# An opening in pieces, block transposes through DRAM in both feed-forwards, and GpSimd as the issuer of their round trips

## The chip, the cores and the metric

The kernel runs on one core of a Trainium2 chip. The metric is the device time of one execution in microseconds (us). TensorE, VectorE, ScalarE, GpSimd and SyncE are the core's engines; each runs its own list of instructions in order and waits on semaphores.

## What is computed

Two transformer layers of batch 1, 256 tokens and width 2048, all in float32. The first: RMS norm, an attention of 16 heads with forget gates ("fox"), a residual, RMS norm, and a gated feed-forward with a causal convolution of width 3 over the tokens. The second: RMS norm, a mixer of two branches (a gated linear recurrence and a banded attention), a residual, RMS norm, a feed-forward with a squared ReLU, and a last norm. The parts that the change touches:

```python
def conv_ffn(h, w_up, conv_w, conv_b, w_down):     # D_FF = 5632
    up = h @ w_up                                   # 2048 x 11264
    padded = jnp.pad(up, ((0, 0), (2, 0), (0, 0)))
    y = conv_b + conv_w[0] * padded[:, 0:seq]
    for tap in range(1, 3):
        y = y + conv_w[tap] * padded[:, tap:tap + seq]
    gate, val = jnp.split(y, 2, axis=-1)
    return (jax.nn.silu(gate) * val) @ w_down

h = h + jnp.square(jax.nn.relu(u @ w_up[l])) @ w_down[l]   # second layer, D_FF_2 = 8192
```

## The kernel before, in words

All weights are streamed from HBM once, as 888 *slots*. A slot is 256 rows by 512 columns (a tile of 128 x 1024, 512 KB). SyncE loads it into one of four buffers `raw` (RING = 4); ScalarE rounds it to `w_hi` (`split`, line 827), VectorE makes the remainder `w_lo` (line 1221), and TensorE multiplies with both: per slot 2 token tiles x 2 row tiles x 3 products (hi x hi, lo x hi, hi x lo; lines 442 to 444) = 12 matmuls of 128 x 512. ScalarE and VectorE run AHEAD = 3 slots before TensorE: at program step p they split slot p + 3, ScalarE when TensorE has finished slot p - 1. SyncE issues a load when VectorE has split the slot four before. The order of everything else on an engine is written out by hand at steps p of each stage, so what stands behind a wait on ScalarE or VectorE are also the splits of later slots.

The activations must lie with the features on the partitions. TensorE turns them: `turn` (line 455) is a group of eight transposes of 128 x 128 into the PSUM banks 4 and 5 (`turn_ps`); `operand` rounds the result on ScalarE (859) and makes the remainder on VectorE (1231).

The *opening*: SyncE loads x in four chunks of 512 columns, each ahead of a slot. ScalarE issues the identity, a table with all gains and convolution taps (`tabs`), the fox gate weights (64-byte rows), a bias and the masks. TensorE turns the tables, then chunk 0 of x, waits for its operand, turns chunk 1, and starts the first slot. In the first fox pass ScalarE issues four DMAs that spread the gates over the partitions, one at each of steps 19 to 22.

*First feed-forward* (`ups1`, `downs`, `pass1`; 11 units of 512 hidden features). A pass of 24 slots is: 8 slots for the gate half of unit i into bank pair 0, 8 for the value half into pair 1, and 8 slots of the down projection of unit i - 1 (`downs`, four column chunks of two slots). Each half is evicted by ScalarE to `stage_q` and turned by TensorE, the gate at step 10 of its pass and the value at step 1 of the next. Then ScalarE computes one tap from PSUM (line 993), VectorE the other two (1395), ScalarE the sigmoid, VectorE the products (1414), and `gated` tells TensorE that the operand of the down projection is ready. In the last pass the value is turned at step 2 of the down slots, and eight more down slots follow for the last unit.

*Second feed-forward* (`ups2`, 16 units): a unit is 8 slots up and 8 slots of the down projection of the unit before. Here the turning is not TensorE's: ScalarE evicts with `by_block`, VectorE squares and transposes blocks of 32 x 32 (1604), one DMA writes 512 KB to DRAM (`turn_rows`) and four of 128 KB read it back with the blocks in place (`block_t`), and ScalarE (1165) and VectorE make the operand. SyncE issues these five DMAs between its weight loads (lines 392 and 401). The first unit uses bank pair 0, and TensorE waits for its eviction (`up2_out`) before the second unit.

GpSimd has little to do: the inverse roots of the norms, some fills, and three DMAs of 1024 KB.

Of the kernel before, what the change touches and what calls it, by code (L numbers as in the profile page):

```python
# [36 lines left out]
P = 128  # L37
# [76 lines left out]
def build_program(nc, a, out):  # L114
    with ExitStack() as ctx:
# [48 lines left out]
        D1_BANKS = [BK[0], BK[1], BK[0], BK[3]]  # L164
# [8 lines left out]
        ident_in, const_in, tab_in, f_kept = sem("ident_in"), sem("const_in"), sem("tab_in"), sem("f_kept")  # L173
        f_in, late_in, level_in, gain_in = sem("f_in"), sem("late_in"), sem("level_in"), sem("gain_in")
# [10 lines left out]
        z1_out, res1_out, up1_out, down1_out = sem("z1_out"), sem("res1_out"), sem("up1_out"), sem("down1_out")  # L185
        z2_out, merged_out, res2_out = sem("z2_out"), sem("merged_out"), sem("res2_out")
# [44 lines left out]
        TN_X, TN_RES1, TN_FFN1, TN_DOWN1 = 0, 4, 8, 8 + 2 * FFN1  # L231
# [67 lines left out]
        tabs = unit(8)[:, 0:5 * P].rearrange("p (k c) -> p k c", k=5)  # L299
        g_T, u_T, s_T = unit(1), unit(2), unit(3)  # L300
        v_pad = scratch[:, 2:4, :].rearrange("p t (h d) -> p t h d", d=P)
# [26 lines left out]
        def _(sp):  # L328
# [10 lines left out]
            def fox_body(R, g, first=False):  # L339
                for k in range(3):  # L340
                    for s in range(SPC):
                        p = k * SPC + s
                        if first and p < NCH:
                            c = slice(p * CW, (p + 1) * CW)
                            sp.dma_start(resid[:, :, c], x[:, :, c]).then_inc(x_in[p], 16)
                        load(R, p, a["w1"], s * SLOT_K * P, g * CW + k * D, wait=not (first and p < RING))
# [12 lines left out]
            def downs(R, p0, w, i, steps={}):  # L359
                for n in range(NCH):  # L360
                    for s in range(JT // SLOT_K):
                        if n * (JT // SLOT_K) + s in steps:
                            steps[n * (JT // SLOT_K) + s]()
# [23 lines left out]
            def turn2_out(i):  # L387

                sp.wait_ge(up2_block, i + 1)
                if i:  # L390
                    sp.wait_ge(up2_back, 64 * i)
                sp.dma_start(turn_rows, block_x).then_inc(up2_sent, 16)

            def turn2_back(i):

                sp.wait_ge(up2_sent, 16 * (i + 1))
                if i:
                    sp.wait_ge(up2_lo, i)
                rows = turn_rows.rearrange("(a p) (b e) -> b p a e", a=4, b=4)
                for b in range(4):  # L400
# [1333 lines left out]
```

## Time and profile before

| | us |
|---|---|
| median of three timed runs (2604.42 to 2606.49) | 2606.37 |
| the profiled execution | 2606.77 |
| its span, first to last instruction | 2604.8 |
| TensorE busy | 2573.1 (99%) |
| VectorE busy | 1596.4 (61%) |
| ScalarE busy | 1248.2 (48%) |
| GpSimd busy | 39.1 (2%) |
| moved by DMA | 495.41 MB, 190 GB/s |

Times in rows are us from the start of the span unless marked ns. PE is TensorE, DVE VectorE, ACT ScalarE, POOL GpSimd, SP SyncE; a q behind the name is the engine's sequencer, which issues DMAs. In a timeline a row is `start, duration, engine, line, operation, written<-read, count`, and in brackets the idle time of the engine before it and what ended it. Matmuls are pipelined: their shown durations overlap, so the distance of two starts tells more than a duration.

### The profile page before, as it was taken

How to read it: one execution, taken by the hardware profiler on the slowest of the kernel's cores; microseconds unless marked ns; L12 is line 12 of the kernel's file. 1: busy time of each engine (PE TensorE's matmuls, PEld its weight loads, DVE VectorE, ACT ScalarE, POOL GpSimd, SP SyncE). 2: the span in 40 equal slices, each digit the busy share in tenths (PEclk: the TensorE clock that was granted, in tenths of full speed). 3: DMA queues.
4: the chain of work that ended last, by engine and by line, in shares of the span. 5: the costliest groups of instructions: out<-in, count | busy, mean ns of one | idle time of the engine just before them, and what ended most of it. 6: DMA issues, size and time to landing. Idle time of an engine off the chain costs nothing.

```text
span 2604.8 us, 32206 instructions
## 1 busy us (share of the span) xinstructions
PE 2573.1 (99%) x11867; PEld 2141.5 (82%) x11867; DVE 1596.4 (61%) x1778; ACT 1248.2 (48%) x1586; POOL 39.1 (2%) x44
## 2 busy tenths in 40 slices
PE   7999999999999999999999999999999999999998
PEld 6888888888888888888888888888888888888886
DVE  4565555666666666675767555456556666666665
ACT  5555555545444444554343545444444444444444
POOL 0000000000000000000000000000000000000000
PEclk9999999999999999999999999999999999999999
DMA  6666555666656666656555655655577676767674
GB/s 199 219 181 174 169 164 176 198 188 187 186 185 191 185 181 186 187 182 186 160 155 164 192 171 163 181 190 186 186 224 220 211 224 213 221 210 224 208 225 157
DMA packets 259509, 495.41 MB, mean 190 GB/s; under 512 B 18060, under 2 KB 27108, under 8 KB 259300
## 3 DMA queue, kind: packets, MB, share of 16 engines
q1 hardware_dynamic: 254720, 486.60, 61.6%
q10 hardware_dynamic: 4019, 4.58, 0.5%
q0 software_dynamic: 688, 3.15, 0.4%
q8 instruction: 51, 0.84, 0.1%
q14 instruction: 31, 0.25, 0.0%
HBM read 483.76 MB, written 10.51 MB: 190 GB/s over the span
## 4 chain that ended last, share of the span: by engine, by line
PE 98%; ACT 0%; DVE 0%; ACTq 0%; DMA 0%; issue 0%; POOL 0%; POOLq 0%; SPq 0%
PE acc L442 31%; PE acc L444 31%; PE acc L443 31%; PE acc L455 2%; PE acc L672 1%; PE acc L515 1%; PE acc L522 0%; DMA raw<-in_w 0%; ACTq L885 0%; PE acc L532 0%; PE acc L544 0%; DVE w_lo L1221 0%; ACT w_hi L827 0%; PE acc L545 0%; PE acc L699 0%
## 5 line engine op out<-in xcount | busy, mean ns | idle before, releaser
L1221 DVE TENSOR_TENSOR w_lo<-raw,w_hi 128x1024 fp32r<-128x1024 f32 x888 | 1080.6, 1223 | 835.8 <-ACT w_hi L827 834.1
L827 ACT ACTIVATE w_hi<-raw 128x1024 fp32r<-128x1024 f32 x888 | 935.8, 1059 | 1060.1 <-PE acc L444 1038.4
L442 PE MATMUL acc<-w_hi,A_hi 128*128 128x512 f32 x1952 | 772.3, 396 | 2.2 <-ACT scratch L837 1.1
L444 PE MATMUL acc<-w_hi,A_lo 128*128 128x512 f32 x1952 | 761.2, 390 | 0.0
L443 PE MATMUL acc<-w_lo,A_hi 128*128 128x512 f32 x1952 | 761.0, 390 | 0.0
L444 PEld LDWEIGHTS acc<-w_hi,A_lo 128*128 128x128 f32 x1952 | 366.9, 188 | 77.2
L442 PEld LDWEIGHTS acc<-w_hi,A_hi 128*128 128x128 f32 x1952 | 367.2, 188 | 76.5 <-issue 1.7
L443 PEld LDWEIGHTS acc<-w_lo,A_hi 128*128 128x128 f32 x1952 | 367.3, 188 | 73.1
L442 PE MATMUL acc<-w_hi,B_hi 128*128 128x512 f32 x800 | 313.6, 392 | 1.5 <-ACT scratch L1181 1.5
L444 PE MATMUL acc<-w_hi,B_lo 128*128 128x512 f32 x800 | 311.5, 389 | 0.0
L443 PE MATMUL acc<-w_lo,B_hi 128*128 128x512 f32 x800 | 311.3, 389 | 0.0
L442 PE MATMUL acc<-w_hi,C_hi 128*128 128x512 f32 x800 | 311.3, 389 | 0.0
L444 PE MATMUL acc<-w_hi,C_lo 128*128 128x512 f32 x800 | 311.2, 389 | 0.0
L443 PE MATMUL acc<-w_lo,C_hi 128*128 128x512 f32 x800 | 311.2, 389 | 0.0
L442 PEld LDWEIGHTS acc<-w_hi,B_hi 128*128 128x128 f32 x800 | 150.2, 188 | 32.5 <-issue 1.9
L444 PEld LDWEIGHTS acc<-w_hi,B_lo 128*128 128x128 f32 x800 | 150.2, 188 | 31.3
L444 PEld LDWEIGHTS acc<-w_hi,C_lo 128*128 128x128 f32 x800 | 150.2, 188 | 31.1
L442 PEld LDWEIGHTS acc<-w_hi,C_hi 128*128 128x128 f32 x800 | 150.2, 188 | 31.1
L443 PEld LDWEIGHTS acc<-w_lo,C_hi 128*128 128x128 f32 x800 | 150.2, 188 | 31.1
L443 PEld LDWEIGHTS acc<-w_lo,B_hi 128*128 128x128 f32 x800 | 150.3, 188 | 30.7
L1249 DVE TENSOR_TENSOR resid<-resid,acc 128x1024 f32<-128x1024 f32 x116 | 141.5, 1220 | 37.9 <-PE acc L444 37.9
L837 ACT ACTIVATE scratch<-acc,small 128x512 f32<-128x512 f32 x108 | 69.3, 686 | 73.8 <-PE acc L444 73.7
(160 smaller groups left out, 1095.3 us busy)
## 6 DMA issues: line engine op xcount, KB each, us to landing
raw<-in_up SPq DMA_DIRECT2D x304, 512.0 KB, 4.5
raw<-in_w SPq DMA_DIRECT2D x272, 512.0 KB, 4.0
raw<-in_down SPq DMA_DIRECT2D x216, 512.0 KB, 4.1
raw<-in_wo SPq DMA_DIRECT2D x64, 512.0 KB, 4.1
raw<-in_wa SPq DMA_DIRECT2D x16, 512.0 KB, 4.9
raw<-in_wb SPq DMA_DIRECT2D x16, 512.0 KB, 4.6
turn_rows<-scratch SPq DMA_DIRECT2D x16, 512.0 KB, 6.5
scratch<-turn_rows SPq DMA_DIRECT2D x64, 128.0 KB, 3.7
```

Source lines behind the costliest of these rows:

```text
L442: pe.matmul(o, hi[:, kt, ts], wh, start=first and kk == 0, stop=False)
L443: pe.matmul(o, hi[:, kt, ts], wl, start=False, stop=False)
L444: m = pe.matmul(o, lo[:, kt, ts], wh, start=False, stop=last and kk == SLOT_K - 1)
L455: m = pe.transpose(turn_ps[:, j * T + t * P:j * T + (t + 1) * P], src(t, j), ident)
L515: m = pe.matmul(o, q[:, t * P:(t + 1) * P], k[:, 0:(t + 1) * P], start=True, stop=True)
L672: m = pe.matmul(o[:, c], s[:, c], t[:, c], start=True, stop=True)
L827: act.activation(w_hi[:, q % RING, :], raw[:, q % RING, :], ACT.Copy).then_inc(w_hi_ready, 1)
L837: m = act.activation(dst[:, t * CW:(t + 1) * CW], acc[:, banks[t], :], func, scale=scale[:, t:t + 1])
L1221: dve.tensor_tensor(w_lo[:, q % RING, :], raw[:, q % RING, :], f32(w_hi[:, q % RING, :]), ALU.subtract).then_inc(w_lo_ready, 1)
L1249: dve.tensor_tensor(v, v, acc[:, banks[0]:banks[1] + 1, :], ALU.add).then_inc(done, 1)
```

## The change

1. *Opening.* Only the 16 rows of the first gain are loaded and turned first; x chunk 0 and slot 0 come in two halves each and ahead of all else; ScalarE and VectorE work on them tile by tile (`early_split`, `early_operand`), and the first slot (`gemm_first`) runs in two halves with two transposes' worth of chunk 0 between them. Chunks 1 to 3 are turned at steps 1 to 3 (before: ahead of the first slot, and at steps 0, 2, 4), the tables at step 4. The fox gate weights, bias and constants are loaded later. The gates are spread by one DMA at step 19 and three at steps 0, 2, 4 of the next pass.
2. *First feed-forward.* The 22 groups of transposes on TensorE go. ScalarE evicts with `by_block`; VectorE transposes 32 x 32 blocks (`turn_blocks`), at step 8 for the gate and behind the split of step 16 for the value; GpSimd issues one DMA out and four back; ScalarE copies the result into place (`up_f`) and the taps are computed from there. The gate's taps move from step 10 to 14. The value's stay at step 1 of the next pass, but at step 5 in the second pass, and in the last pass they move from step 2 to 5 of the down slots. The down projection uses the bank pairs 2 and 3 alone.
3. *Second feed-forward.* GpSimd issues the round trips in place of SyncE. The first unit uses bank pair 3, so TensorE no longer waits for its eviction.

The diff, cut:

```diff
-        D1_BANKS = [BK[0], BK[1], BK[0], BK[3]]
+        D1_BANKS, D1_LAST = [BK[2], BK[3], BK[2], BK[3]], [BK[0], BK[1], BK[0], BK[3]]
...
+            def first_loads():
+                h = CW // 2
+                sp.dma_start(resid[:, :, 0:h], x[:, :, 0:h]).then_inc(x_early, 16)
+                sp.dma_start(raw[:, 0, 0:CW], a["w1"][0:P, 0:CW]).then_inc(w_early, 16)
+                sp.dma_start(raw[:, 0, CW:2 * CW], a["w1"][P:2 * P, 0:CW]).then_inc(landed[0], 16)
+                sp.dma_start(resid[:, :, h:CW], x[:, :, h:CW]).then_inc(x_in[0], 16)
...
+            def gemm_first():
+                for kk in range(SLOT_K):
+                    pe.wait_ge(early_hi, kk + 1)
+                    pe.wait_ge((w0_hi, w_hi_ready)[kk], 1)
...
+                    if kk == 0:
+                        pe.wait_ge(x_in[0], 16)
+                        turn_pair(2, turned)
+                m.then_inc(slot_done, 1)
...
+                if p in (1, 2, 3):
+                    pe.wait_ge(x_in[p], 16)
+                    turn(chunk_of_resid(p), TN_X + p)
+                if p in (2, 4):
+                    pe.wait_ge(turn_dve, TN_X + 1 + p // 2)
+                if p == 4:
+                    turn_tabs()
...
-                    elif p == 1:
-                        pe.wait_ge(up1_out, 2 * i)
-                        turn(halves(stage_q), TN_FFN1 + 2 * i - 1)
-                    if p == 10:
-                        pe.wait_ge(up1_out, 2 * i + 1)
-                        turn(halves(stage_q), TN_FFN1 + 2 * i)
+                    elif p % SPC == 0:
+                        pe.wait_ge(up1_out, 2 * i - 1 + p // SPC)
...
+                        if isinstance(g, int) and p in (0, 2, 4):
+                            spread_gates(1 + p // 2)
...
+            def conv_tap(i, half, dst):
+                n = 2 * i + half
+                act.wait_ge(up1_back, 64 * (n + 1))
...
+                act.activation(up_f.rearrange("p (m a q) -> p m a q", m=JT * TT, a=4), from_quads(up_t),
+                               ACT.Copy).then_inc(up1_flat, 1)
...
-                    if p == 10:
+                    if p == 14:
...
-                if q == 2:
+                if q == 5:
                     act.wait_ge(gated, FFN1 - 1)
                     conv_value(FFN1 - 1)
...
+            def turn_blocks(n, first=False):
+                dve.wait_ge(up1_out, n + 1)
+                if not first:
+                    dve.wait_ge(up1_sent, 16 * n)
+                dve.transpose(up_x, up_q).then_inc(up1_block, 1)
...
+                    if p == SPC:
+                        turn_blocks(2 * i, first)
...
-            downs(R4 - 4, 0, D1_BANKS, down1_out, steps=lambda q: value_steps(q - 2, FFN1 - 1, B_hi, B_lo))
+            downs(R4 - 4, 0, D1_BANKS, down1_out, steps=lambda q: value_steps(q - 5, FFN1 - 1, B_hi, B_lo),
+                  turn=2 * FFN1 - 1)
...
+            for n in range(2 * FFN1):
+                pool.wait_ge(up1_block, n + 1)
+                if n:
+                    pool.wait_ge(up1_back, 64 * n)
+                pool.dma_start(up_rows, up_x).then_inc(up1_sent, 16)
+                pool.wait_ge(up1_sent, 16 * (n + 1))
+                if n:
+                    pool.wait_ge(up1_flat, n)
+                for b in range(4):
+                    pool.dma_start(up_t[32 * b:32 * (b + 1), :].rearrange("p (a e) -> p a e", a=4),
+                                   up_by_quad[b]).then_inc(up1_back, 16)
...
+            for i in range(FFN2):
+                pool.wait_ge(up2_block, i + 1)
...
+                pool.dma_start(turn_rows, block_x).then_inc(up2_sent, 16)
```

## Rows read from the trace of the kernel before

**Rows 1.** The page: busy time of TensorE, and the last chain by engine.
```profile
PE 2573.1 (99%) x11867; PEld 2141.5 (82%) x11867; DVE 1596.4 (61%) x1778; ACT 1248.2 (48%) x1586; POOL 39.1 (2%) x44
...
PE 98%; ACT 0%; DVE 0%; ACTq 0%; DMA 0%; issue 0%; POOL 0%; POOLq 0%; SPq 0%
```

**Rows 2.** Stretches: busy time per engine, clock, DMA share, GB/s.
```profile
81.80:94.80 13.00, 13.00 (x59) 10.78 (x58) 6.34 (x5) 4.28 (x5) 0.44 (x1) 1.00 0.99 363
529.50:596.60 67.10, 67.10 (x306) 55.73 (x305) 43.59 (x47) 33.12 (x38) 0.00 (x0) 1.00 0.61 187
2047.90:2091.40 43.50, 43.50 (x193) 36.05 (x192) 27.45 (x23) 19.10 (x19) 0.00 (x0) 1.00 0.71 206
```

**Rows 3.** Waits of TensorE, whole run: total us, times, longest.
```profile
PE acc L468 <- DMA scratch<-in_rows: 8.6, 1, 8.6
PE acc L455 <- DVE A_lo L1231: 6.3, 1, 6.3
PE acc L442 <- ACT scratch L1181: 1.5, 1, 1.5
```

**Rows 4.** Timelines of the opening: ScalarE, VectorE, TensorE.
```profile
11.08 1.28 ACT L888 ACT_TABLE_LOAD   x1 [11.08 <-issue]
...
14.12 1.55 ACT L859 ACTIVATE A_hi<-acc,gain 128x256 fp32r<-128x256 f32 x4
...
15.70 1.66 DVE L1231 SCALAR_TENSOR_TENSOR A_lo<-acc,gain,A_hi 128x256 fp32r<-128x256 f32 x4 [0.23 <-ACT A_hi L859]
...
19.10 0.78 PE L442 MATMUL acc<-w_hi,A_hi 128*128 128x512 f32 x1
...
22.66 0.41 PE L444 MATMUL acc<-w_hi,A_lo 128*128 128x512 f32 x1
...
39.05 0.39 PE L442 MATMUL acc<-w_hi,A_hi 128*128 128x512 f32 x1
```

**Rows 5.** DMA issues: count, KB each, median us to landing.
```profile
const<-in_const ACTq DMA_DIRECT2D x1, 64.0 KB, 4.7
...
turn_rows<-scratch SPq DMA_DIRECT2D x16, 512.0 KB, 6.5
scratch<-turn_rows SPq DMA_DIRECT2D x64, 128.0 KB, 3.7
...
scratch<-in_rel POOLq DMA_DIRECT2D x2, 1024.0 KB, 7.8
...
scratch<-in_gain_out POOLq DMA_DIRECT2D x1, 1024.0 KB, 4.8
```

**Rows 6.** Timeline of TensorE at the two late starts.
```profile
96.40 0.50 PE L442 MATMUL acc<-w_hi,A_hi 128*128 128x512 f32 x1 [1.15 <-ACT scratch L837]
...
1917.19 0.49 PE L442 MATMUL acc<-w_hi,B_hi 128*128 128x512 f32 x1 [1.48 <-ACT scratch L1181]
```

**Rows 7.** Timelines of VectorE and SyncE, one trip of the second feed-forward.
```profile
2116.03 1.25 DVE L1604 STREAM_TRANSPOSE scratch<-scratch 128x1024 f32<-128x1024 f32 x1
...
2126.57 1.75 SPq L401 DMA_DIRECT2D scratch<-turn_rows  x4
```

**Rows 8.** Groups by line, ScalarE and VectorE: count, busy us, mean ns.
```profile
L1165 ACT ACTIVATE C_hi<-scratch 128x1024 fp32r<-128x1024 f32 x12 | 12.5, 1042 | 0.0
...
L1395 DVE SCALAR_TENSOR_TENSOR scratch<-acc,conv,scratch 128x255 f32<-128x255 f32 (+1 forms) x16 | 6.6, 476 | 2.0 <-ACT scratch L993 1.7
...
L993 ACT ACTIVATE scratch<-acc,conv 128x256 f32<-128x256 f32 x8 | 3.9, 564 | 0.1
```

**Rows 9.** Timeline of GpSimd: two small operations, two DMA issues.
```profile
63.61 1.11 POOL L1648 TENSOR_TENSOR small<-small 128x8 f32<-128x8 f32 x1 [20.82 <-DVE small L1329]
...
1436.10 0.20 POOL L1648 TENSOR_TENSOR small<-small 128x8 f32<-128x8 f32 x1 [117.51 <-DVE small L1525]
...
1438.43 1.09 POOL L1681 DMA_DIRECT2D scratch<-in_rel  x1
...
1903.89 0.60 POOL L1697 DMA_DIRECT2D scratch<-in_gain_out  x1
```

More of the change, by code:

```diff
@@ L228, in build_program @@
         U2 = rounds(SPC)
[L231 removed]
+        TN_X, TN_RES1, TN_DOWN1 = 0, 4, 8
         TN_HG = TN_DOWN1 + 4
@@ L299, in build_program @@
         tabs = unit(8)[:, 0:5 * P].rearrange("p (k c) -> p k c", k=5)
+        mix_rows = unit(8)[0:KT, 5 * P:6 * P]
         g_T, u_T, s_T = unit(1), unit(2), unit(3)
+        up_q, up_x, up_t, up_f = unit(0), unit(5), unit(6), unit(7)
+        up_rows = nc.dram_tensor("up_rows", (P, 1024), F32, kind="Internal").ap()
         v_pad = scratch[:, 2:4, :].rearrange("p t (h d) -> p t h d", d=P)
@@ L462, in chunk_of_resid, with turn_pair @@
                 return lambda t, j: resid[:, t, c * CW + j * P:c * CW + (j + 1) * P]
-            pe.wait_ge(ident_in, 16)
-            pe.wait_ge(tab_in, 16)
-            for k, (rows, col) in enumerate([(G_END, 0)] + [(88, P * (1 + k)) for k in range(4)]):
-                m = pe.transpose(acc[:, 6 + k // 4, (col % CW):(col % CW) + rows], tabs[0:rows, k, :],
-                                 ident[0:rows, 0:rows])
-            m.then_inc(tabs_turned, 1)
+            def turn_pair(j0, done):
+                for j in (j0, j0 + 1):
+                    for t in range(TT):
+                        m = pe.transpose(acc[:, 4 + j, t * P:(t + 1) * P], chunk_of_resid(0)(t, j), ident)
+                m.then_inc(done, 1)
@@ L561, in fox_pass @@
                         pe.wait_ge(z1_out, 3 * g + 1)
+                    if first and p == 0:
+                        gemm_first()
+                        continue
                     gemm(R, p, A_hi, A_lo, s, BK[c % 2], s == 0, s == SPC - 1, late, z1_half if s == SPC - 1 else None)
@@ L799, in ups2 @@
                             pe.wait_ge(turn_dve, TN_RES2 + 4)
-                    elif p == 0:
+                    elif p == 0 and not isinstance(i, int):
                         pe.wait_ge(up2_out, i)
-                    gemm(R, p, B_hi, B_lo, p, BK[0], p == 0, p == SPC - 1)
+                    gemm(R, p, B_hi, B_lo, p, BK[3 if first else 0], p == 0, p == SPC - 1)
             ups2(R7, 0, first=True)
@@ L887, in _ @@
-            act.wait_ge(tabs_turned, 1)
-            act.activation(gain[:, :], acc[:, 6, 0:G_END], ACT.Copy)
-            act.activation(conv[:, 0:3, :], acc[:, 6, P:4 * P].rearrange("p (k c) -> p k c", k=3)[:, :, 0:88], ACT.Copy)
-            chain.link(act.activation(conv[:, 3, :], acc[:, 7, 0:88], ACT.Copy))
-            act.activation(fq_scale, gain[:, G_FQ:G_FQ + 1], ACT.Copy, scale=-float(P) ** -0.5).then_inc(tabs_kept, 1)
-            split(0, -AHEAD)
-            operand(TN_X, A_hi, 0, G_MIX)
+            act.dma_start(mix_rows, a["rows"][0:KT, :]).then_inc(mix_in, 16)
@@ L1432, in downs @@
                         split(R, p0 + q)
+                    if turn is not None and q == 0:
+                        turn_blocks(turn)
                     if steps:
```

266 lines of the change are left out of this document (163 added, 103 removed).

## The prediction

> **What bounds the kernel now.** I read the page first, then the waits of TensorE, then its timeline. The page says that TensorE is busy 2573.1 us of the span of 2604.8 and that the chain that ended last is TensorE to 98% [rows 1]. Busy time alone could hide bubbles, so I took the stretch of one whole unit of the second feed-forward: 16 slots (one 128 x 1024 weight load, 12 matmuls each) in 43.5 us, 2.720 us a slot [rows 2]. The 888 slots make 2415 us; the other 190 us are other matmuls, transposes and the few waits. TensorE waited 8.6, 6.3 and 1.5 us, three times less than that, and no more [rows 3]. So a change can gain where it takes an instruction off TensorE or one of these waits; that SyncE issues only weight loads gains nothing by itself, since no weight load after the opening holds TensorE except at 94.9 us, which is another matter (below). And the change can lose wherever a new round trip comes back too late.
>
> The profiled execution took 2606.8 us, 2.0 more than its span; the median of the three timed runs is 0.4 lower. I sum against 2606.4.
>
> **Part 1, the opening.** Before, the first transposes wait for the table of gains (8.6 [rows 3]), ScalarE loads its function table at 11.08, splits the whole first slot and then takes the whole first operand (14.12, 1.55 long), VectorE follows (15.70, 1.66), and the first slot starts at 19.10. Its first eight matmuls take until 22.66, 0.445 us each, near twice the later 2.720 / 12 = 0.227 [rows 4]: the spacing of the 1.2 GHz level. Slot 6 starts at 39.05 [rows 4].
> After: identity (64 KB) lands 4.7 us after its issue [rows 5], which is among the first of the program, so at about 5.4; one transpose of 16 rows, ScalarE sees it at 5.9. Table load 1.28, copy of the gains 0.24: 7.5. Half a split 0.6: 8.1. One operand tile 0.4: 8.55. TensorE's first matmul is then at about 8.6 (19.10 before). The two halves of x and w before it are 256 KB each and are ahead of everything else on SyncE's queue; I take them as there by then. From here the chain is new and less generous: slot 0 with a pair of transposes inside at half speed ends at 14.2; slot 1 waits for its split (VectorE 15.3) and ends at 18.1; chunk 2 may be transposed only when chunk 1's operand is done, 1.55 on ScalarE and 1.66 on VectorE after the transposes: 18.6; slot 2 ends 22.2; chunk 3 in the same way at 23.0; slot 3 ends 26.6; the tables' five transposes 0.6; slots 4 and 5 end at 32.6. So slot 6 starts at 32.6 where it started at 39.05: **-6.5 us**. Bounds: if the table load runs before the wait, -7.7; if the small loads land 2 us late, -4.5. What follows (fox gate weights, constants) is loaded later than before; the fox weights are issued about 28 and wanted about 33 to 40 by the f-path, on cover of two slots.
> The spreading of the gates moves from four DMAs in a row (768 KB each, one a slot) to one, and then one in two slots of the next pass. Before, the DMA engines were 99% busy at 363 GB/s from 81.8 to 94.8 [rows 2] and TensorE then stood idle 1.15 us ahead of 96.40 [rows 6]. Per two slots the new order asks 768 KB and two loads, 1.8 MB in 5.9 us, 305 GB/s: I count the whole gap as gone, **-1.2** (between 0 and -1.2).
>
> **Part 2, the first unit of the second feed-forward** uses another bank, so the wait of TensorE for the eviction goes. It stood idle 1.48 us ahead of 1917.19 [rows 6]: **-1.5**. Nothing is late behind it: the next split was ready two slots ahead.
>
> **Part 3, the first feed-forward.** Removed: 22 groups of eight transposes. One pass of 24 slots with two groups takes 67.10 us [rows 2]; 24 x 2.720 = 65.28; so a group costs 0.905, and 22 cost **-19.9**. TensorE has no other cover there, this is all on the path.
> Added, per group: VectorE's transposition of 32 x 32 blocks (1.25 us as in the second feed-forward [rows 7]), a DMA out, four back, and a ScalarE copy of 1.04 us [rows 8]. The engines have room (VectorE 43.6 and ScalarE 33.1 busy of 67.1 [rows 2]); order and latency decide.
> *The deadline of the gate.* The accumulation ends at the end of slot 8 of a pass (call it 0). Evictions 1.3, then ScalarE's split of the next slot, VectorE's (1.22) and only then the block transposition: 4.9. ScalarE takes the result behind its 14th split, at 6 x 2.72 + 1.2 = 17.5. **The round trip has 12.6 us.**
> *What a trip takes.* From SyncE: 6.5 out [rows 5], then four issues in 1.75 [rows 7] and 3.7 from an issue to its landing [rows 5], about 5.0 to 6.0 for the set: 11.5 to 12.5. From GpSimd the trace has only three DMAs, of 1024 KB: two kinds, the issue 1.09 and 0.60 long [rows 9], landing 7.8 and 4.8 us after the issue [rows 5]. On GpSimd's queue a trip does not stand behind a weight load, as it does on SyncE's. For 512 KB I estimate 3.3 to 6 us out; back, three issues (1.8 to 3.3) and then 2.5 to 3.7 for the last, 4.3 to 7. In all 8 to 13, and I take **10.5**, nearer to the lower of these than to SyncE's.
> The Trainium skill speaks against this (DMA: Bandwidth & Descriptors, section SWDGE vs HWDGE vs iDMA): plain copies belong on SyncE or ScalarE, whose descriptors come from hardware, and in the section on latency the first byte takes about 1 us from GpSimd and 0.6 us otherwise. By that page alone the trip would be some 5 x 0.4 = 2 us over SyncE's, 14, past the deadline. The trace neither shows nor excludes it.
> *Behind the gate, every pass.* From ScalarE's 14th split on: copy 1.0, four taps 1.9, VectorE's eight taps 3.4 [rows 8], sigmoid 1.1, then ScalarE's 15th split and VectorE's product and split; from 1.2 after slot 14 this comes to 11.2, while slot 18 wants its weights at 4 x 2.72 = 10.9. (Before, the same chain stood at slot 10 without the copy and with 0.9 us of transposes as slack.) About **0.3 in each of 10 passes, +3.0** (0 to 5).
> *The first unit*, whose value half is consumed at slot 21 of the second pass: eviction at 16 comes behind the gate chain, block transposed at +6.4, back at +16.9 with 10.5; ScalarE stood ready from +14.8 (slot 5 of the next pass). Behind its wait stand the weight splits of the next slots: copy, taps and VectorE's taps (together 6.2) and a split 1.2 make slot 25 ready at +24.6 to 25, about on time, slot 26 about 1.8 late, and the gate of the same pass, evicted late, comes back 2 us late at slot 30: together **+4.5**, 2 us more for each us of the trip.
> *The last unit.* Its value half is complete at slot 16 of the last pass, and TensorE needs the product at slot 24, 21.8 us later. Eviction behind the gate chain +5.4; split 16 stands ahead of the block transposition: +8.8. Trip 10.5: +19.3. Then copy 1.1, taps 1.9, VectorE's taps 3.4, a residual addition 1.2, a split 1.2, product 1.2, ScalarE's copy 1.1 and split 1.0, VectorE's split 1.2 and difference 1.2: 14. Ready at +33.4: **TensorE waits 11.7 us**, 1 us more for each us of the trip. Before, the same value was turned by TensorE at slot 18 and was ready in time (TensorE has no such wait [rows 3]). This is the step that eats the gain. After the idle stretch of 6.3 us in the opening [rows 3] eight matmuls ran near half as fast [rows 4]: 3.56 - 8 x 0.227 = **+1.7**, and this one is longer.
>
> **Part 4, the trips of the second feed-forward** from GpSimd. In a steady unit the block is ready 3.9 us after slot 8 and wanted 2 slots into the next unit, 27 us on: free with any trip here. The last unit consumes at its 14th slot, 17.5 us after: trip of 13.6 free. Counted **0**.
>
> **Sum:** -6.5 - 1.2 - 1.5 - 19.9 + 3.0 + 4.5 + 11.7 + 1.7 = -8.2; 2606.4 - 8.2 = **2598.2 us**.
>
> **Rivals.**
> A shorter trip, 8 us: the last wait is 9.2, the first unit's cost is almost gone (0 to 0.5), and with the 1.2 us that an early table load gives the opening the sum is -16: **2591**. For it: the 4.8 us for 1024 KB; against: four issues from GpSimd have no row.
> A trip of 11.5 to 13, or an opening that gains only 2 to 3 us: within 0.2%, about **2603**. For it: SyncE's 11.5 to 12.5.
> **Slower: the gate's trip misses its deadline in every pass.** Place: ScalarE behind its 14th split, where the splits of the weights queue behind the wait. Up to 12.6 us the sum is only -8.2 + 3 x 2.1 = -1.9; beyond, each us costs 10 times in the steady passes, twice in the first and once in the last, 13 us. At 14 us: +16, **2622**. It decides from 13 us on. For it: the 1.09 us issues and 7.8 us; against: half the bytes.
> **Slower still: GpSimd is held by VectorE while it issues.** A small GpSimd operation took 0.20 us alone and 1.11 beside VectorE [rows 9]. Were each of five issues 1.2 longer, the trip would be 16.5: **2655**. The Trainium skill (SBUF — State Buffer, section Who interferes with whom) says that VectorE in its two-port modes blocks GpSimd, while an operation with two SBUF inputs contends with GpSimd's reads only; the feed-forward's VectorE operations are of the latter kind, so by that page descriptors are written unhindered.
> That SyncE's queue gains by losing the trips: no row for it, 0.
>
> **How the numbers follow.** The forecast (trips of 9.3 to 11.5) has a chance of 0.44, the short trip 0.18, the case within 0.2% 0.18, the missed deadline 0.16, the held GpSimd 0.04. A measurement of this kernel can tell about 0.2%, 5.2 us, from no change. So faster 0.62, same 0.18, slower 0.20. The range reaches from the short trip with a little more, 2589, to a trip of 13.5, 2616: left out are the last case and about half of the missed deadline.
>
> **What would show it.** Right: no transposes from a scratch tile in the first feed-forward; TensorE's first 512-column matmul near 8.6; slot 6 near 32.6; passes of 65.3 to 65.8 us; one wait of 10 to 13 us before the last eight slots of the first feed-forward, released by VectorE's difference; trips of 9 to 12 us. Wrong: passes above 66 us mean a missed deadline; no long wait at the end means that I have the order of the last value wrong; and a first matmul after 11 means that the small loads were late.

## The result and the profile after

The changed kernel takes 2650.76 us (median of four runs, 2649.13 to 2651.8); the kernel before, timed beside it, 2606.43 (2604.42 to 2606.93). The ratio is 1.0171 with a 95% interval of 1.0153 to 1.0189: slower by 44.3 us, where I had forecast 8 us faster and a range that ends at 2616.

The length of each stage, from the first 512-column matmul of its first slot to that of the next stage, in us:

| stage (slots) | before | after |
|---|---|---|
| first such matmul | 19.10 | 7.01 |
| fox passes (96) | 299.92 | 302.18 |
| FFN1 unit 0 (16) | 45.35 | 44.45 |
| FFN1 pass 1 (24) | 67.09 | 81.62 |
| FFN1 passes 2 to 9, mean | 67.09 | 69.95 |
| FFN1 pass 10 (24) | 68.00 | 84.81 |
| FFN1 last chunk (8) | 25.72 | 27.08 |
| FFN2 unit 0 and pass 1 (24) | 67.98 | 66.21 |
| all FFN1 | 742.9 | 797.6 |

What isn't listed is equal to within 0.4 us. FFN1 lost 54.7 us; the rest gained 11.3 (spans 2604.8 and 2648.2).

The page of the changed kernel: busy time, the last chain by engine, and the DMA issues of the trips (count, KB each, median us to landing).

```profile
PE 2573.4 (97%) x11692; PEld 2130.7 (80%) x11692; DVE 1620.0 (61%) x1801; ACT 1270.5 (48%) x1610; POOL 143.4 (5%) x234
...
PE 70%; issue 16%; DMA 11%; POOL 1%; DVE 1%; ACT 1%; POOLq 0%; ACTq 0%; SPq 0%
...
up_rows<-scratch POOLq DMA_DIRECT2D x22, 512.0 KB, 5.3
scratch<-up_rows POOLq DMA_DIRECT2D x88, 128.0 KB, 5.5
```

TensorE had 98% of the last chain [rows 1] and has 70% now; DMA, 0% before, has 11%. The transposes are gone (11867 to 11692 instructions) and TensorE's busy time is the same as before. That doesn't mean that they were free: after its stalls TensorE runs slower for some matmuls (granted clock of the run 0.988; 0.87 from 1177.7 to 1190.0), and a busy time counts those longer. It happens in the middle of FFN1 too. In five of the passes 2 to 9 the granted clock falls to 0.50, the lower of its two levels (1.2 GHz), for 3.4 us or twice as long, each time around the end of a stall of 2.0 to 3.0 us; after stalls of 2.6 us in pass 5 and 2.9 in pass 8 it doesn't. Pass 3 has most of it (window, length, busy time of PE, PEld, DVE, ACT, POOL, granted clock, DMA share, GB/s):

```profile
603.60:675.28 71.68, 68.72 (x290) 55.97 (x288) 45.74 (x49) 35.04 (x40) 5.47 (x10) 0.95 0.69 211
```

In the mean of passes 2 to 9 TensorE is idle for 2.9 us and its work takes 1.8 us more than the 65.28 of 24 slots; 1.2 of these 1.8 lie in the stretches at 0.50. "issue", 16% of the last chain, is time for which the profile shows no cause. What TensorE waits for (us in all, times, longest):

```profile
PE acc L438 <- DVE w_lo L1285: 37.0, 16, 5.4
PE acc L438 <- DVE B_lo L1497: 16.7, 1, 16.7
PE acc L496 <- DMA scratch<-in_rows: 5.1, 1, 5.1
PE acc L438 <- issue: 0.8, 1, 0.8
```

Of the three waits of [rows 3] none is left as it was. The first line is new: TensorE waits for the low half of a weight, on an engine that is 61% busy. VectorE waits for ScalarE's high half there, and ScalarE, in the same list of waits, stood 32.9 us in 13 times for a trip's way back and 38.4 us in 11 times for VectorE's taps. One pass, number 5, shows how these go together. ScalarE (start, length, engine, line, operation, idle before it and what ended that):

```profile
783.40 1.06 ACT L852 ACTIVATE w_hi<-raw 128x1024 fp32r<-128x1024 f32 x1 [1.66 <-PE acc L440]
786.06 1.06 ACT L1044 ACTIVATE scratch<-scratch 128x1024 f32<-128x1024 f32 x1 [1.60 <-DMA scratch<-up_rows]
787.37 2.08 ACT L1049 ACTIVATE scratch<-scratch,conv 128x256 f32<-128x256 f32 x4 [0.25 <-ACT scratch L1044]
793.12 1.06 ACT L1078 ACTIVATE scratch<-scratch 128x1024 f32<-128x1024 f32 x1 [3.67 <-DVE scratch L1482]
794.09 1.04 ACT L852 ACTIVATE w_hi<-raw 128x1024 fp32r<-128x1024 f32 x1
```

and VectorE, GpSimd and TensorE in the same stretch:

```profile
770.47 1.24 DVE L1472 STREAM_TRANSPOSE scratch<-scratch 128x1024 f32<-128x1024 f32 x1
...
772.01 0.56 POOL L1772 DMA_DIRECT2D up_rows<-scratch  x1 [34.15 <-DVE scratch L1472]
777.21 2.18 POOL L1777 DMA_DIRECT2D scratch<-up_rows  x4 [4.64 <-DMA up_rows<-scratch]
...
796.84 0.50 PE L438 MATMUL acc<-w_hi,C_hi 128*128 128x512 f32 x1 [2.60 <-DVE w_lo L1285]
```

The block is turned at 771.71. ScalarE ends its 14th split at 784.46: the trip had 12.75 us, and I had said 12.6. It took until 786.06, 14.35. So ScalarE stands 1.60 us for the trip, then copies and does its taps, then stands 3.67 us for VectorE's taps, and does not split a weight from 784.46 to 794.09, 9.6 us, while the ring holds three slots, 8.2 us. TensorE, idle for 2.60 us, goes on at 796.84.

From the issue of the out to the landing of the last of the four backs, the 11 gate trips took 12.9 to 14.5 us, mean 14.0, and the 11 value trips 13.8 to 16.1, mean 15.3. ScalarE had to wait for all 11 gates (0.5 to 4.9 us), and of the values only for the first (5.5) and the last (7.4): the other nine came in time. The end of FFN1, on ScalarE and on TensorE:

```profile
1163.24 1.06 ACT L1044 ACTIVATE scratch<-scratch 128x1024 f32<-128x1024 f32 x1 [7.40 <-DMA scratch<-up_rows]
...
1177.69 0.79 PE L438 MATMUL acc<-w_hi,B_hi 128*128 128x512 f32 x1 [16.73 <-DVE B_lo L1497]
...
1181.12 0.39 PE L440 MATMUL acc<-w_hi,B_lo 128*128 128x512 f32 x1
```

The last value's trip ends 7.40 us after ScalarE was ready for it and TensorE waits 16.73 us.

### The profile page after: what moved, and what is told of

Same layout as the page of the kernel before. It is cut to its first block, busy times and chain, and to the rows that moved or that the text cites. A ratio compares the mean times of both kernels' runs of the same rounds, so it can differ in the third digit from the quotient of the medians.

```text
span 2648.2 us, 32718 instructions
## 1 busy us (share of the span) xinstructions
PE 2573.4 (97%) x11692; PEld 2130.7 (80%) x11692; DVE 1620.0 (61%) x1801; ACT 1270.5 (48%) x1610; POOL 143.4 (5%) x234
## 4 chain that ended last, share of the span: by engine, by line
PE 70%; issue 16%; DMA 11%; POOL 1%; DVE 1%; ACT 1%; POOLq 0%; ACTq 0%; SPq 0%
PE acc L438 22%; PE acc L440 22%; PE acc L439 22%; DMA scratch<-up_rows 6%; DMA up_rows<-scratch 4%; POOL scratch L1777 1%; PE acc L694 1%; PE acc L546 1%; PE acc L451 1%; PE acc L553 0%; PE acc L563 0%; PE acc L575 0%; DVE w_lo L1285 0%; DMA raw<-in_w 0%; ACT w_hi L852 0%
## 5 line engine op out<-in xcount | busy, mean ns | idle before, releaser
L438 PEld LDWEIGHTS acc<-w_hi,A_hi 128*128 128x128 f32 x1948 | 366.6, 188 | 88.2 <-DVE w_lo L1285 13.2
L438 PE MATMUL acc<-w_hi,C_hi 128*128 128x512 f32 x800 | 316.9, 396 | 28.4 <-DVE w_lo L1285 28.4
L438 PE MATMUL acc<-w_hi,B_hi 128*128 128x512 f32 x800 | 314.4, 393 | 16.7 <-DVE B_lo L1497 16.7
L438 PEld LDWEIGHTS acc<-w_hi,C_hi 128*128 128x128 f32 x800 | 152.7, 191 | 64.6 <-DVE w_lo L1285 32.6
L1482 DVE SCALAR_TENSOR_TENSOR scratch<-scratch,conv 128x255 f32<-128x255 f32 (+1 forms) x176 | 73.4, 479 | 82.6 <-ACT scratch L1049 80.1
```

The source lines that it names most:

```text
L438: pe.matmul(o, hi[:, kt, ts], wh, start=first and kk == 0, stop=False)
L1482: m = dve.scalar_tensor_tensor(out=v, in0=up_f[:, j * T:(j + 1) * T - d], scalar=conv[:, 2 - d, bass.ds(col, 1)], in1=v, op0=ALU.mult, op1 ...
```

## The experiments

**The theories.** *D, the deadline*: a trip that lasts 14 to 15 us keeps ScalarE from the weight splits. *T, the traffic*: the trips' packets delay the weight loads (ScalarE waited 99.7 us in 50 times for up-weights). *Q or S, the order*: copy, taps, VectorE's taps and sigmoid in one piece on ScalarE's queue are too long by themselves. *G*: the trip is that long because GpSimd issues it. Up-steps are steps 0 to 15 of a pass and down-steps its last eight, counted from 0. The kernels of runs 4 and 10 were timed four times, the others once; the seven executions of the kernel before that were timed beside run 1 spread from 2605.1 to 2609.3 us, so differences of a few us between single runs say nothing, while a pass without a stall repeats to 0.1 us from run to run.

**1. No trips.** Edit:

```diff
-                act.wait_ge(up1_back, 64 * (n + 1))
+                act.wait_ge(up1_block, n + 1)
-                act.activation(up_f..., from_quads(up_t),
+                act.activation(up_f..., from_quads(up_x),
```
and GpSimd's FFN1 loop left out; VectorE waits for ScalarE's copy, and no more for a landing, before it writes the next block.

> The changed kernel with FFN1's 22 round trips through DRAM left out: ScalarE copies straight from VectorE's block-transposed tile as soon as VectorE has written it, so the blocks are not moved between partition groups and the output is not the reference's. Everything else, the order of every queue included, is as in the changed kernel. Theory D (deadline: a trip lasts 14 to 15 us, ScalarE stands in the wait for it in front of the weight splits that TensorE needs): the stalls go, passes 2 to 9 of FFN1 fall from 69.95 us to between 65.3 and 65.8, pass 1 from 81.6 to about 66, pass 10 from 84.8 to at most 70, the whole to about 2580 (2575 to 2586). Theory T (the trips' packets hold up the weight loads): the same, since the packets are gone too. Rival Q (the new order of ScalarE's and VectorE's queues itself, with the gate's chain at step 14, is what starves TensorE): the passes stay above 67 and the whole above 2600.

Measured: 2599.7 us; passes 2 to 9 at 66.82, pass 1 at 66.77, pass 10 at 73.87. The big part of the loss goes with the trips, but a pass isn't at 65.3. Without any trip it still costs 1.5 us over 24 x 2.720, so Q holds for that part. ScalarE and TensorE in pass 5:

```profile
760.37 2.08 ACT L1049 ACTIVATE scratch<-scratch,conv 128x256 f32<-128x256 f32 x4 [0.25 <-ACT scratch L1044]
766.12 1.06 ACT L1078 ACTIVATE scratch<-scratch 128x1024 f32<-128x1024 f32 x1 [3.67 <-DVE scratch L1482]
...
769.84 0.50 PE L438 MATMUL acc<-w_hi,C_hi 128*128 128x512 f32 x1 [0.89 <-DVE w_lo L1285]
```

The same 3.67 us for VectorE's taps, no trip ahead of them, and TensorE still 0.89 idle behind. The three expected numbers of D (passes at 65.3 to 65.8, pass 10 at most 70, the whole near 2580) were all missed. In pass 10 it is because TensorE waits 7.6 us for the last value even here: ScalarE takes that value at down-step 5 and not sooner, whether there is a trip or none.

**2. The traffic without the wait.** Edit: as run 1, but GpSimd's loop stays, without its wait for ScalarE's copy.

> As the run without trips, but GpSimd makes all 22 trips, out and back, with the same bytes and descriptors as in the changed kernel; only nobody in FFN1's chain waits for what they bring back (ScalarE copies from VectorE's tile; the output is not the reference's). VectorE and ScalarE wait for the last trip once, after FFN1's last slot. Theory D alone: what counts is the wait, so this run equals the one without trips within 4 us (about 2582) and passes 2 to 9 stay at 65.3 to 65.8. Theory T: the weight loads land in 6 to 9 us beside the trips instead of 4.3, ScalarE waits for them as before, and passes 2 to 9 stand 1.5 us or more above those of the run without trips, the whole 15 us or more above it. If both hold, it lies between: 66 to 67.5 a pass.

Measured: 2608.2 us, 8.5 above run 1. Passes 2 to 9 run from 66.79 to 68.83, mean 67.37: 0.55 us a pass over run 1. The traffic costs something, in some passes, but it is a fifth of what passes 2 to 9 lose (69.95 - 66.82 = 3.1); 2.6 us come from the wait and from the lower clock behind it (in run 2 the clock stays at 1.00 in passes 1 to 9). The answer is between the two, nearer to D.

**3. More time for the gate's trip.** Edit, on ScalarE and VectorE alike (and the banks of the down-projection, with TensorE's waits for them):

```diff
-                    if p == 14:
-                        ... gate: taps, sigmoid, product
+                if q == 2:            # in the down-steps
+                    gate_steps(i)
-        D1_BANKS = [BK[2], BK[3], BK[2], BK[3]]
+        D1_BANKS = [BK[2], BK[3], BK[2], BK[1]]
```

> The changed kernel, all of it computed, with more time for the gate's trip: ScalarE and VectorE do the gate's taps, sigmoid and product after the split of down-step 2 instead of after the split of up-step 14 (unit 0's after step 1 of pass 1), 4 slots or 10.9 us later; the fourth chunk of a down-projection uses the banks of the value so that VectorE's later additions don't hold TensorE. Trips and traffic are unchanged. Theory D alone: the gate's trip has about 23 us instead of 12.6 and is hidden, passes 2 to 9 take 65.3 to 66.0, pass 1 about 66.5, pass 10 still 76 to 80 (the value's chain of the last unit is as it was), the whole about 2650.8 - 9*4.2 - 15 - 6 = 2595 (2588 to 2600). Theory T as well: late weight loads remain and still show, passes 2 to 9 at 66.7 to 68, the whole 2603 to 2618. If neither, the passes stay at 69 to 70 and the whole above 2635.

Measured: 2601.3 us, 49.5 less than the changed kernel with all the trips and bytes in it; gate trips of 13.2 to 15.2 us. Passes 1 to 9 take 66.75 to 66.83, as without trips. So a trip costs nothing while it is inside its time, and here neither does the traffic; why the same bytes cost 0.55 us a pass in run 2 was not told apart. Both numbers expected by D were too low, the whole (2588 to 2600, measured 2601.3) and the pass (65.3 to 66.0, measured 66.8), by the same 1.5 us a pass as in run 1.

One thing changed that was not expected. The gate trips are as long as before, mean 14.5, but the value trips, from the same GpSimd, take 9.4 to 11.2 us, mean 10.6, where the changed kernel's took 15.3. The outs are nearly alike (4.8 and 5.4 us in the mean); the four backs take 5.5 us and not 9.6. What differs beside them is the weights that move in the same time. The changed kernel from 777.21 to 786.10 (a gate's backs), then this one from 773.93 to 779.54 (a value's backs); queue, packets, MB, share of 16 engines, q0 being GpSimd's trips and q1 SyncE's weights:

```profile
q1 hardware_dynamic: 974, 1.88, 71.3%
q0 software_dynamic: 192, 0.52, 25.9%
...
q0 software_dynamic: 192, 0.52, 39.7%
q1 hardware_dynamic: 285, 0.54, 25.8%
```

That is 0.21 MB of weights per us beside the long backs and 0.10 beside the short. Over all of GpSimd's trips in this kernel, the changed one and runs 2, 5, 9 and 10, the 86 backs of over 8 us had 1.4 MB of weights or more beside them and the 25 of under 6 us 0.9 or less. How long a trip from GpSimd takes is thus not a property of its queue alone.

**4. Opening and FFN2 alone.** Edit: the kernel before with all hunks of the diff except FFN1's.

> The kernel before with the new opening and the new FFN2 (GpSimd's trips, the peeled first pass, unit 0's banks) alone; FFN1 is the kernel before's, with TensorE's transposes. The traces say that the opening is worth -9.8 us by the end of the fox stage and FFN2's first unit -1.8, the tail +0.3: 2606.4 - 11.3 = 2595 (2592 to 2599), ratio 0.9957. Then all of the loss, +54 to +56 us, is FFN1's. If the opening's gain were eaten later by an engine that is now behind, or GpSimd's trips in FFN2 cost something, it would be 2600 or more.

Measured: 2595.34 us (2595.13 to 2596.0), ratio 0.9958 (0.9941 to 0.9974). All of the loss is FFN1's, and the two other parts are worth 10.8 us beside a kernel before of 2606.14. FFN2's passes take 43.52 us with GpSimd's trips and 43.5 with SyncE's [rows 2].

**5. The sigmoid one split later.** Edit to run 3 (VectorE's product goes with the sigmoid; the gated value's copy and difference likewise come a step later):

```diff
                 if q == 2:
-                    conv_tap(i, 0, g_T); act.wait_ge(conv_dve, 2 * i + 1); act.activation(s_T, g_T, ACT.Sigmoid)
+                    conv_tap(i, 0, g_T)
+                if q == 3:            # after the next weight split
+                    act.wait_ge(conv_dve, 2 * i + 1); act.activation(s_T, g_T, ACT.Sigmoid)
```

> The run with more time for the gate's trip (2601.3 us, passes 2 to 9 at 66.8), and one thing more: ScalarE no longer stands in its queue for VectorE's taps. It makes the sigmoid one step later, behind the next weight split, and the gated value's copy one step later too; all is computed. Theory S (serial chain: in the run without trips ScalarE made no split between 758.1 and 767.1 us, 3.67 us of it waiting for VectorE's taps, and the ring's three slots of 2.72 us don't cover that; it is what is left of the recurring stall, 1.5 us a pass): passes 1 to 9 fall to 65.3 to 65.6, the whole to 2601.3 - 9*1.4 = 2588.7 (2586 to 2592). Theory T (late weight loads make it): the passes stay above 66.4 and the whole above 2597.

Measured: 2587.5 us. Passes 1 to 9 take 65.28 each, which is 24 x 2.720: nothing is left of the stall in them, with gate trips of 12.3 to 15.4 us and value trips of 9.2 to 10.9 (mean 10.5). Pass 10 still takes 74.09. Pass 5 of this kernel:

```profile
713.98:779.26 65.28, 65.28 (x290) 54.05 (x288) 45.27 (x51) 35.20 (x40) 5.50 (x10) 1.00 0.73 225
```

and the same pass of the changed kernel:

```profile
744.80:813.31 68.51, 65.88 (x289) 53.90 (x288) 45.52 (x49) 35.05 (x40) 5.48 (x10) 1.00 0.69 206
```

The work of every engine is the same to 0.6 us; only the order differs. At 225 GB/s the weights are in time, so T isn't needed for anything in these passes.

**6. No trips, sigmoid one split later.** Edit: run 1, with sigmoid and product at up-step 15 instead of 14.

> The run without trips (2599.7 us, passes 2 to 9 at 66.8; the blocks are not moved, so the output is not the reference's), with the gate's sigmoid and product put one step later (up-step 15 instead of 14), behind the next weight split. Theory S: ScalarE's stretch without a split is 3.7 us shorter, passes 1 to 9 fall to 65.3 to 65.9, the whole to about 2588 (2585 to 2592); the 0.33 us at up-step 5 stays, since the gated value's copy is not moved. If the stall came from the copy that flattens the block (0.98 us of ScalarE more than in the kernel before), the passes would fall by nothing or by less than 0.5 us: 66.3 or more, the whole 2595 or more.

Measured: 2588.5 us, passes 2 to 9 at 65.66: 1.16 less than run 1, as theory S had it. What is left is 0.33 us in slots 5 and 6, as expected from the value's copy, which was not moved.

**7. A longer trip.** Edit: each block is written out twice, one after the other.

> The changed kernel with each of FFN1's 22 trips made longer: GpSimd writes the block out twice, the second time after the first has landed, and only then fetches it back; all is computed. An out took 5.3 us from issue to landing, so a gate's trip goes from 14.0 to about 19.3 us. Theory D (past its deadline each microsecond of a trip is one of the pass): passes 2 to 9 go from 69.95 to about 75 (73 to 77), pass 1 from 81.6 to about 97 (three trips follow each other in it), pass 10 from 84.8 to about 95, the whole about 2650.8 + 8*5 + 15 + 10 = 2716 (2700 to 2735). Theory T alone (bytes, not the wait): 22 more writes of 512 KB, a quarter to a third more traffic, passes at most 1 us longer, the whole below 2665.

Measured: 2735.0 us, just beyond what D expected. Gate trips of 17.7 to 20.9 us, mean 19.6, in place of 14.0; passes 2 to 9 at 77.5 (69.95 + 7.5 for 5.6 us of trip), pass 1 at 96.0, pass 10 at 94.7. TensorE's wait for `w_lo` is 108.3 us:

```profile
PE acc L439 <- DVE w_lo L1286: 108.3, 21, 9.6
```

Past the deadline a microsecond of trip is more than one of the pass. Of the 7.5 us a pass 6.3 are idle time of TensorE and 1.2 slower matmuls (granted clock 0.93 to 0.96 in these passes). In most passes both trips now come late (ScalarE waited for one 20 times, 108.9 us), so this run lengthens two waits in a pass and not one alone.

**8. The same trips issued by SyncE.** Edit, in place of GpSimd's loop:

```diff
+            ups1(R, i, {0: lambda: turn1_out(2 * i - 1), 2: lambda: turn1_back(2 * i - 1)})
+            downs(R, 2 * SPC, a["down1"], i - 1, {0: lambda: turn1_out(2 * i), 2: lambda: turn1_back(2 * i)})
```

> The changed kernel with FFN1's 22 trips issued by SyncE instead of GpSimd, between its weight loads (the gate's out ahead of the load of down-step 0, its back ahead of down-step 2, the value's ahead of the next pass's up-steps 0 and 2); SyncE's passes are written out for it; all is computed, every other queue is as in the changed kernel. Theory G (it is GpSimd's software queue that makes the trip 14 to 15 us): the trip takes about 12, as SyncE's own trips in FFN2 of the kernel before (12.0 to 12.9), inside the 12.6 us that ScalarE leaves it, passes 2 to 9 fall from 69.95 to 67 or 67.5, the whole to about 2650.8 - 8*2.7 - 8 - 5 = 2616. Theory D/T (two 512 KB moves through DRAM beside a weight stream of 512 KB each 2.72 us take 12 to 15 us whoever issues them): the trip stays at 12 to 14.5 and the passes at 68.5 to 70.5, the whole between 2635 and 2655. If SyncE's waits for the block hold up its weight loads, the passes rise above 71.

Measured: 2618.1 us, where G expected 2616. The DMA issues of the trips on its page:

```profile
up_rows<-scratch SPq DMA_DIRECT2D x22, 512.0 KB, 5.5
scratch<-up_rows SPq DMA_DIRECT2D x88, 128.0 KB, 4.0
```

In the median the out lands no sooner than GpSimd's (5.5 and 5.3 us); a back does, 4.0 against 5.5. Gate trips take 11.3 to 13.2, mean 12.2, value trips 10.8 to 12.8, mean 11.9: 1.8 and 3.4 us less than GpSimd's. The mean gate trip is then inside the 12.6 us, and passes 2 to 9 fall to 67.2, within 0.4 of the run without trips. SyncE waited for a block 22 times, 0.8 us at the longest, and for an out to land 22 times, 2.5 us at the longest; the weight loads stand behind these waits, and the passes don't show it.

So with SyncE as the issuer, at the places of the changed kernel, the gate's trip is mostly in time, and that is worth 32.7 us. It is one edit and two differences: the queue, and the order, since SyncE holds back its next weight loads until an out has landed and the four backs are issued, and GpSimd's trips hold back no load. That GpSimd's queue by itself makes a trip long is not shown, and run 3 speaks against it: its value trips from GpSimd, 10.6 us, are shorter than SyncE's 11.9 here.

**9. The changed kernel with the sigmoid one split later.**

> The changed kernel with one edit: the gate's sigmoid (ScalarE) and its product (VectorE) come at up-step 15 instead of 14, behind the next weight split, so that ScalarE doesn't stand still for VectorE's taps. The gate's trip is waited for at step 14 as before. In the runs without trips the same edit took 1.15 us from each pass. If the parts of the stall simply add (serial chain 1.5 us, traffic 0.5, wait for the trip 2.6 in the mean of passes 2 to 9), passes 2 to 9 go from 69.95 to about 68.7 and the whole to 2650.8 - 10*1.2 = 2639 (2632 to 2645). If the ring was empty anyway when the trip came back, so that only the last of the two counts, the edit brings less than 3 us in all.

Measured: 2628.4 us; the edit brings 22.3 us, twice what adding up gave. Passes 2 to 9 fall by 2.2 us to 67.7, pass 1 by 5.0. The parts do not add. TensorE's idle time in passes 2 to 9 falls from 2.9 to 1.3 us a pass, and the granted clock, at 0.50 in stretches of five of these passes before, stays at 1.00 in all eight. The clock explains part of what adding up missed; why the idle time fell by 1.6 and not by 1.2 was not tried.

**10. All of it, and the last unit as before.** Edit: run 5, but unit 10 of FFN1 is turned by TensorE, at up-step 10 and down-step 2, as in the kernel before; 20 trips remain.

> The deferred kernel of this batch with unit 10, the last of FFN1, turned by TensorE as in the kernel before (its gate at up-step 10, its value at down-step 2, 2 * 0.9 us of TensorE); 20 trips are left; all is computed. Pass 10 took 75.1 us in the run with more time for the gate, 68.0 in the kernel before, because nothing is left after it to hide a trip behind. Expected: pass 10 at 66.5 to 68.2, FFN1's last chunk at 25.4 instead of 27.3, the whole about 2588.7 - 7.5 - 1.8 = 2579 (2576 to 2583), ratio 0.990. By theory T, with passes at 66.8 still: 2590 to 2593.

Measured: 2577.16 us (2576.96 to 2577.61), ratio to the kernel before 0.9888 (0.9872 to 0.9905). Pass 10 takes 67.09, the last chunk 25.43, passes 1 to 9 65.28 each. It is 29.3 us faster than the kernel before and 73.6 faster than the changed one. TensorE's longest wait, and all that is left of the one for `w_lo`:

```profile
PE acc L496 <- DMA scratch<-in_rows: 4.6, 1, 4.6
...
PE acc L438 <- DVE w_lo L1333: 0.4, 1, 0.4
```

The trips are now off the path altogether: 20 x 0.905 = 18.1 us of transposes saved, against 18.2 measured from run 4 to this one.

## Why the prediction was wrong, point by point

- **The step that failed is the trip, "I take 10.5".** Measured: 14.0 for a gate, 15.3 for a value. The way out was right: 3.3 to 6 us expected, 4.8 to 6.1 measured. The way back was not: "4.3 to 7" expected, and the four backs landed 7.1 to 10.6 us after the first was issued. GpSimd's slower issue is a small part of that (0.55 us each, 2.18 for four, where four took SyncE 1.75). I had reasoned from [rows 9] and [rows 5] that GpSimd's queue stands behind no weight load, and gave the weights that move beside it no price. That is what is missing: where the weights moved at 0.21 MB per us the backs took 8.9 us, where they moved at 0.10 MB per us 5.6 (run 3), and with such backs, for the values of runs 3 and 5, a trip from GpSimd did take 10.6 and 10.5 us. That the weights are the reason is read from such pairs and was not tried by itself. My range of 8 to 13 holds 1 of the 22 trips of the changed kernel. The nearest rows of the same size and shape, SyncE's trips, I had put at 11.5 to 12.5 from medians; trip by trip the trace of the kernel before has 11.3 to 14.0, mean 12.6, which is the deadline itself, so the rows at hand already spoke against a trip that is in time.
- **The Trainium skill's warning was right in its result and not in its way.** From the first byte of about 1 us against 0.6 (DMA: Bandwidth & Descriptors, section Latency and other measured facts) I had estimated 14 us, 0.4 us for each of five DMAs. That met the gate's 14.0, and neither the value's 15.3 nor the 10.6 of run 3. Beside run 8 the gate's out took 0.4 us more from GpSimd, the step to the first back 0.3 and the backs 1.1; the value's out took 0.3 less and its backs 3.4 more. So the same 0.4 us five times over is not what the trace shows, and that the sum came to 14 is in part luck. The page's advice, plain copies from SyncE or ScalarE (section SWDGE vs HWDGE vs iDMA), is borne out by run 8 for this place.
- **The deadline was right**: 12.6 us predicted, 12.75 in the timeline, and in run 8 trips of 12.2 us are nearly free in passes 2 to 9 (67.2, and 66.8 without trips).
- **So the rival "the gate's trip misses its deadline in every pass" came true**, in the place it named, but at 2651 and not at 2622. I had given it a chance of 0.16. Its slope, 13 us per us of trip, was near: run 7 took 84.3 us more for gate trips 5.6 and value trips 4.6 us longer. What it had too low is the level at 14 us. About 24 of the missing 29 us lie in passes 2 to 9, which lost 4.7 us each over 65.28 where the rival has 0.3 + 1.4: the chain behind the wait took 1.5 and not 0.3 (run 1), the traffic 0.55 and not 0 (run 2), and the rest, the wait with the lower clock behind it, 2.6 and not 1.4. Run 9 shows that these parts don't simply add, so the split is only rough.
- **The slow clock, +1.7 once**, is the second term that was mis-sized. After the last wait it was 1.6, as forecast (below). But the granted clock fell to 0.50 after the stalls of pass 1 and of five other passes as well, and I had counted nothing there: TensorE's work took 4.7 us more in pass 1 than in pass 1 of run 1, and 1.2 us a pass in the mean of passes 2 to 9, some 14 us in all. (The eight slow matmuls from 19.10 of [rows 4], from which I took the term, have a granted clock of 1.00 in the profile; that they ran at the lower level was read from their distance alone, 0.445 us, near the 0.43 us measured at 0.50 after the last wait.)
- **"Behind the gate, +0.3 in each pass"** was mis-sized: 1.5 us a pass in run 1, without any trip. The chain from the start of slot 14 to the wanted weight took 11.9 us there (757.91 to 769.84), not 11.2, against 10.9 available, the matmuls after the stall came slower, and a second loss of 0.33 us in slots 5 and 6 had not been seen at all. I had priced each operation and not the gaps between them, such as 0.25 us between a copy and the taps that read it. In run 3 the trip's deadline is gone and the 1.5 us remain; in run 5 they are gone too.
- **The last unit, +11.7 and 1 us more for each us of trip**: the trip was 15.6, so 16.8 by my own slope, and the wait is 16.7. Right in place, and wrong only by the trip; the slope holds for long trips (13.0 us of waiting at a trip of 12.2 in run 8, where it gives 13.4) and not for short ones, since 7.6 us remain in run 1 without any trip. TensorE's first eight matmuls after it, from 1177.69 to 1181.12, took 3.43 us where 8 x 0.227 = 1.82 are usual, at a granted clock of 0.50, so the 1.7 us for the slow clock was 1.6.
- **The first unit, +4.5 and 2 us more for each us**: at a trip of 14.6 that is 12.7; pass 1 is 16.3 us over its 65.28, of which 1.5 is the recurring chain, so 14.8; of these some 4.7 are matmuls at the lower clock, for which I had no term, so that the 12.7 is near by luck.
- **The 22 groups of transposes, 19.9**: right. Passes fall from 67.09 to 65.28 in runs 5 and 10, 1.81 for two groups.
- **Opening, gate gap and FFN2, -6.5 - 1.2 - 1.5 = -9.2**: measured -10.8 in run 4. Slot 6 starts at 30.67, not at 32.6, and was at 39.05 [rows 4], 1.9 us sooner than forecast, mostly because the first matmul came at 7.01 and not at 8.6:

```profile
1.77 1.28 ACT L909 ACT_TABLE_LOAD   x1 [1.77 <-issue]
...
7.01 1.22 PE L482 MATMUL acc<-w_hi,A_hi 128*128 128x512 f32 x2 [0.63 <-ACT A_hi L912]
```

  The table load, 11.08 before [rows 4], ran ahead of the wait, at 1.77: the case for which I had named -7.7, and slot 6 came 8.4 us sooner. From 81.8 to 94.8 us the DMA share fell from 0.99 [rows 2] to 0.82 (0.80 from 70 to 94.8, since the program is 12 us ahead there), and the stop of 1.15 us ahead of 96.40 [rows 6] is gone.
- **FFN2's trips from GpSimd, 0**: right.
- **GpSimd held by VectorE** would have given 2655, near the measured time, and it isn't what happened: the 88 issues of backs took 0.55 to 0.58 us each and the 22 of outs 0.56 in the median, 0.75 at most, beside VectorE at 61%. The Trainium skill (SBUF — State Buffer, section Who interferes with whom) says that an operation of VectorE with two SBUF inputs contends with GpSimd's reads and not with its writes; the weights' remainder is such an operation, and the trace agrees. A time can be hit by the wrong mechanism.

What stays open: why GpSimd's four backs land later than SyncE's where many weights move. Issue time explains 0.4 us of it (2.18 against 1.75 us for four). GpSimd's packets are of 4096 bytes and SyncE's of 1024 for the same bytes, and GpSimd's go by a queue of their own while SyncE's stand in one with the weights; which of these counts was not told apart.

## What to carry to other kernels

When a step leaves the engine that was waited for and goes by a longer way round, compute the deadline on the engine whose queue holds the wait, and compare it with the slowest trip the nearest rows show, not with a hoped-for one: here trips 1.4 us past the gate's deadline, with the first and the last unit's, cost 50 us by run 3, because weight splits stood behind the wait. Read such a trip one by one and with what moves beside it, not as a median. Then put the wait where there is slack (a later step, one split in between) before tuning the trip; the same 14 us trips cost nothing in passes 1 to 9 of run 5. A stall also costs what TensorE loses at the lower clock behind it. And leave the last round of a loop to the short way, since nothing is left there to hide a long one behind.

## What was not expected of the hardware

- The time of a DMA depended here on what was beside it at least as much as on who issued it. GpSimd's 512 KB outs took 3.2 to 3.3 us in FFN2, all 16, where the weights moved 0.08 to 0.16 MB beside them (SyncE's, in the kernel before, 5.1 to 7.4 beside 0.7 to 1.7 MB), and 4.8 to 6.1 in FFN1; in the one shown, 0.90 MB of weights moved in the same time. The DMA of the changed kernel in the two windows (queue, packets, MB, share of 16 engines; then the issue and its landing), first 1986.51 to 1989.70 us, then 772.01 to 777.00:

```profile
q0 software_dynamic: 144, 0.52, 47.2%
q1 hardware_dynamic: 54, 0.11, 15.0%
...
turn_rows<-scratch POOLq DMA_DIRECT2D x1, 512.0 KB, 3.2
...
q1 hardware_dynamic: 458, 0.90, 58.9%
q0 software_dynamic: 144, 0.52, 28.9%
...
up_rows<-scratch POOLq DMA_DIRECT2D x1, 512.0 KB, 4.9
```

  The Trainium skill (DMA: Bandwidth & Descriptors, section Anatomy of one DMA — SWDGE (gpsimd) path) fits 2.0 us + bytes / 436 GB/s for one DMA from GpSimd, 3.2 us for 512 KB. The trace agrees with it to 0.1 us in FFN2, where the DMA is almost alone, and shows 1.6 to 2.9 us more beside the weight stream of FFN1. The whole trips of FFN2 took about as long from either engine, 11.4 to 14.4 us from GpSimd (mean 13.2) and 11.3 to 14.0 from SyncE (mean 12.6).
- The way back, 512 KB in four DMAs, took 4.6 to 5.8 us for the values in run 5 and 7.0 to 10.9 for the gates in the same passes. In pass 5 the weights moved 1.85 MB beside the gate's backs and 0.46 beside the value's. That the weights are what makes the one slow is argued from such pairs and was not tried by itself.
